# Order of the parts inside an attention step of a two-model transformer kernel

## The reference

```python
# first model: 8 heads of 64; with 256 tokens there is one block, so causal softmax
p = softmax(where(causal, (q*scale) @ k.T, -1e30)); out = p @ v
attn = head_rms_norm(out, g)

# second model, layer 0: 8 heads, two score maps of 64 each, values of 128
w = softmax(q1 @ k1.T) - lam * softmax(q2 @ k2.T); o = rmsnorm(w @ v) * (1 - lam_init)

# second model, layer 1: 8 query heads of 128 on 2 key/value heads, no mask
o = softmax(q @ k.T) @ v
```

## Time and profile before

| what | value |
|---|---|
| timed runs, median (lowest to highest) | 1385.19 us (1384.85 to 1385.59) |
| profiled execution | 1380.57 us |
| its span | 1378.8 us |
| TensorE busy | 1148.3 us, 83% |
| VectorE busy | 611.7 us, 44% |
| ScalarE busy | 540.8 us, 39% |
| chain that ended last | PE 58%, DMA 24%, DVE 9%, ACT 7%, issue 2% |
| first / second / third attention | about 164 to 206 / 755 to 842 / 1110 to 1146 us |
| experts | about 240 to 700 us |

### The profile page before, as it was taken

One profiled execution on the slowest core, in us unless ns is written; L12 is line 12 of the kernel. 1 busy time (PEld: TensorE's weight loads), 2 busy tenths in 40 slices (PEclk: granted clock), 3 DMA queues, 4 the chain that ended last, 5 costly groups with the idle time before them and its releaser, 6 DMA issues.

```text
span 1378.8 us, 22374 instructions
## 1 busy us (share of the span) xinstructions
PE 1148.3 (83%) x9627; PEld 916.8 (66%) x9627; DVE 611.7 (44%) x1363; ACT 540.8 (39%) x1203; POOL 0.2 (0%) x4
## 2 busy tenths in 40 slices
PE   6989998866656666555689989999999979999997
PEld 4867668543333444333357758899998758899997
DVE  4564664210100111110065756665555865655554
ACT  4554553211100110110154655555554754555553
POOL 0000000000000000000000000000000000000000
PEclk9999998998887898987899999999999999999999
DMA  9895846899999999999978646645545664655520
GB/s 392 340 357 222 350 190 244 332 427 428 428 424 428 424 427 427 427 426 427 428 311 323 217 182 224 247 182 184 184 145 210 235 236 183 245 184 184 184 92 31
DMA packets 29569, 397.53 MB, mean 288 GB/s; under 512 B 3480, under 2 KB 4888, under 8 KB 5400
## 3 DMA queue, kind: packets, MB, share of 16 engines
q1 hardware_dynamic: 29032, 395.72, 71.8%
q10 hardware_dynamic: 432, 0.30, 0.1%
HBM read 394.97 MB, written 1.05 MB: 287 GB/s over the span
## 4 chain that ended last, share of the span: by engine, by line
PE 58%; DMA 24%; DVE 9%; ACT 7%; issue 2%; ACTq 0%; DVEq 0%
PE ps L141 58%; DMA ring<-in_w 12%; DMA mem<-in_w 11%; DVE mem L141 4%; DVE memr L141 3%; ACT mem L141 3%; ACT memr L141 3%; DMA ring<-in_wpk 1%; DVE small L141 1%; DMA posi<-in_pos 1%; ACT L141 0%; ACT rowb L141 0%; DVE x L141 0%; DVE mcol L141 0%; ACTq L141 0%
## 5 line engine op out<-in xcount | busy, mean ns | idle before, releaser
L141 PE MATMUL ps<-memr 128*128 128x256 f32 (+1 forms) x4680 | 668.6, 302 | 17.9 <-DVE memr L141 17.9
L141 PEld LDWEIGHTS ps<-memr 128*128 128x128 f32 x4680 | 610.7, 192 | 62.4 <-DVE memr L141 27.7
L141 DVE TENSOR_TENSOR memr<-ring,memr 128x512 fp32r<-128x512 f32 x440 | 297.8, 691 | 245.3 <-ACT memr L141 242.0
L141 ACT ACTIVATE memr<-ring 128x512 fp32r<-128x512 f32 x440 | 268.3, 627 | 220.0 <-PE ps L141 212.3
L141 PE MATMUL ps<-mem 128*32 128x256 f32 (+4 forms) x2232 | 266.8, 407 | 59.9 <-DMA mem<-in_w 35.2
L141 ACT ACTIVATE mem<-ps 128x256 f32<-128x256 f32 (+5 forms) x307 | 121.3, 407 | 421.4 <-PE ps L141 419.4
L141 PEld LDWEIGHTS ps<-mem 128*32 128x32 f32 (+2 forms) x2232 | 172.8, 147 | 117.8 <-issue 59.5
L141 PE MATMUL ps<-ring,mem 128*32 128x256 f32 x1536 | 140.6, 432 | 75.6 <-DMA mem<-in_w 39.0
L141 PEld LDWEIGHTS ps<-ring,mem 128*32 128x32 f32 x1536 | 72.2, 124 | 122.4 <-issue 99.3
L141 DVE TENSOR_TENSOR mem<-mem,ps 128x256 f32<-128x256 f32 (+1 forms) x76 | 31.8, 418 | 270.7 <-ACT mem L141 270.6
L141 DVE COPY mem<-ps 32x256 f32<-32x256 f32 (+2 forms) x81 | 38.2, 471 | 114.9 <-PE ps L141 113.9
(11 more groups left out here) (91 smaller groups left out, 380.4 us busy)
## 6 DMA issues: line engine op xcount, KB each, us to landing
ring<-in_wpk SPq DMA_DIRECT2D x89, 2048.0 KB, 8.1
mem<-in_w SPq DMA_DIRECT2D x48, 2048.0 KB, 32.0
ring<-in_w SPq DMA_DIRECT2D x48, 2048.0 KB, 30.4
mem<-in_wpk SPq DMA_DIRECT2D x1, 2048.0 KB, 10.5
ring<-in_wpk SPq DMA_DIRECT2D x2, 1024.0 KB, 5.1
x<-in_x SPq DMA_DIRECT2D x2, 512.0 KB, 5.6
out_dram<-mem SPq DMA_DIRECT2D x4, 256.0 KB, 2.2
cst<-in_cst SPq DMA_DIRECT2D x1, 944.0 KB
```

The costliest lines, as they stand in the source:

```text
L141: ins = o[1](*o[2], **o[3])
```

## The change

In both generators the calls inside a step are put in another order. Before: scores, weigh, turn_e, values, finish. After, in the first attention: values, turn_e, finish, weigh, scores; in the second model's: values, turn_e, finish, weigh, scores as well. The conditions, the heads that each call works on, the parts themselves and the places of the steps between slabs stay.

```diff
@@ -1048,16 +1048,16 @@
                 uu_free[u] = c_r[ch]
 
             for s_ in range(12):
+                if 3 <= s_ < 11:
+                    values(s_ - 3)
+                if 2 <= s_ < 10:
+                    turn_e(s_ - 2)
+                if s_ >= 5 and s_ % 2:
+                    finish((s_ - 5) // 2)
+                if 1 <= s_ < 9:
+                    weigh(s_ - 1)
                 if s_ < 8:
                     scores(s_)
-                if 1 <= s_ < 9:
-                    weigh(s_ - 1)
-                if 2 <= s_ < 10:
-                    turn_e(s_ - 2)
-                if 3 <= s_ < 11:
-                    values(s_ - 3)
-                if s_ >= 5 and s_ % 2:
-                    finish((s_ - 5) // 2)
                 yield
 
 
@@ -1711,16 +1711,16 @@
             def attention():
 
                 for s_ in range(21):
+                    if s_ >= 4 and s_ % 2 == 0 and s_ < 20:
+                        values(s_ // 2 - 2)
+                    if 2 <= s_ < 18:
+                        turn_e(s_ - 2)
+                    if s_ >= 5 and s_ % 2:
+                        finish((s_ - 5) // 2)
+                    if 1 <= s_ < 17:
+                        weigh(s_ - 1)
                     if s_ < 16 and s_ % 2 == 0:
                         scores(s_ // 2)
-                    if 1 <= s_ < 17:
-                        weigh(s_ - 1)
-                    if 2 <= s_ < 18:
-                        turn_e(s_ - 2)
-                    if s_ >= 4 and s_ % 2 == 0 and s_ < 20:
-                        values(s_ // 2 - 2)
-                    if s_ >= 5 and s_ % 2:
-                        finish((s_ - 5) // 2)
                     yield
 
             at_ = attention()
```

## The result

The changed kernel takes 1396.52 us (median of 6 runs, 1394.26 to 1398.04), the old one beside it 1385.39 us. The ratio is 1.0077, 95% interval 1.0064 to 1.0089: 10.7 us slower (8.9 to 12.3); the two medians lie 11.1 apart. The profiled execution took 1396.07 us (span 1394.2).

What follows compares the result with a forecast made beforehand. Outside the transfer-paced expert part, time was taken to be lost where TensorE waits. Second attention +2.5, third +3.9, first +0.3 sum to +6.7 us on the 1385.19 median: 1391.9, range 1386.0 to 1397.0.

Steps and rivals of the forecast that it cites:

- rival A: More slow clock: one extra slow stretch each in the second and third attention, 1.4 us each, 1394.7 us; chance 0.18.
- Step 9 and 10 of the second attention: Scaling runs behind finish and ends at 806.95; step 10's transposes wait 2.4 us for it.
- The slab behind it: Second attention, step 10: transposes 0.2, scores 1.07, slab 1.65, ending at 809.95 instead of 808.4; 1.5 us lost.
- It is in the old time, and I leave one in the new: Second attention: one half-clock stretch behind steps 11 and 12, costing 1.4 us, stays in the new time.
- Step 12: Second attention: values at 812.1 after the turned copy, scaling behind finish at 815.25, scores end near 816.6; lag 1.0 us.
- The closed loop: Third attention: one head's chain from scores to transposes takes 4.6 us, against 2.45 between scores(4) and scores(5) before.
- Step 2's lag: First attention: scores now start behind the wait for scaling(0), before 1.09 us; loses 0.8 us.
- so the cadence stays: First attention: a pair of steps takes VectorE and ScalarE about as long in either order.
- the 1.40: First attention, step 9: the wait of 1.40 us shrinks, since 0.8 us of values go ahead of the transposes.
- Rivals B and C: B: faster, finish and values freed, 1380.8 us, chance 0.08. C: nothing to measure, gains and losses cancel, 1385.2, chance 0.12.
- The 0.71 us waits: Second attention: the finish product's 0.71 us waits for the square go, since the square no longer stands behind the exponentials.
- PSUM's banks: Banks taken in rotation change their order of use; taken as 0, bounds -0.5 and +1 us.

Runs made afterwards that it cites:

- e7: The whole change plus one to three idle-time products, results unread, ahead of TensorE's long waits in all three attentions; 9.0 us slower than the old kernel, ratio 1.0065.
- e8: The whole change, but step 12 of the second attention keeps the old order; 10.5 us slower than the old kernel, ratio 1.0076.
- e9: The old order plus one idle-time product ahead of step 11's transposes and one ahead of step 12's values, second attention; 2.8 us faster than the old kernel, ratio 0.9980.
- e1: The old kernel with only the first attention put in the changed order; 3.5 us slower, ratio 1.0025.
- e4b: All three attentions ordered values, turn, scaling, finish, scores: the change with scaling ahead of finish; 7.9 us slower than the old kernel, ratio 1.0057.
- e5: All three attentions ordered scores, values, turn, finish, scaling: scores first, the rest reversed; 3.5 us slower than the old kernel, ratio 1.0025.
- e2: The old kernel with only the second attention put in the changed order; 5.3 us slower, ratio 1.0038.
- e6: The old order with values ahead of scores in the first and second attention, except the second's step 12; 2.2 us slower than the old kernel, ratio 1.0016.
- e3: The old kernel with only the third attention put in the changed order; 3.9 us slower, ratio 1.0028.
- e10: As e9, plus values ahead of scores in the second attention except steps 11 and 12; 2.4 us faster than the old kernel, ratio 0.9983.

## Why the prediction was right, and where it was short

The side was right, and so was the place: slower, in the attentions. 1396.5 lies in the range, near its upper end, but above the forecast's own high end (near 1395): it is inside by the room left above rival A, not by the sum. The forecast of +6.7 us was 4 us short, and rival A (+9.5) came closest. By the timed runs of one attention each, +0.3 became +3.5, +2.5 became +5.3, and +3.9 was met.

- **Step 9 and 10 of the second attention.** Right, by 0.04 us for the end of the scaling and 2.01 us for a wait put at 2.4.
- **The slab behind it.** I put transposes, scores and slab of step 10 at 2.9 us. They took 811.37 + 2.78 - 809.51 = 4.6. The step that failed is "It is in the old time, and I leave one in the new": in the second attention there is a slow stretch behind each of the three waits of 2 us or more, not one in all. e7's trace puts the clock at 4.4 us of the second attention's 5.8 and 2.6 of the third's 6.1 (by e8's trace of the same code it would be 1.1); e9 shows such a price once, 1.7 us, and there the timed runs agree.
- **Step 12.** I let values wait for the turned copy only and missed that values(4) also wait for the copies of the value projection's second half, which ScalarE has behind the finish chain. So values came last and not the scaling: in the change the copies end at 817.74 and values start at 817.89. Transposes and scores queued behind them, and the units start 22.0 us behind step 8's start, forecast 816.6 - 797.83 = 18.8. In e7 it is 819.63 - 800.16 = 19.5, so 2.5 of the 3.2 us are clock. The other 0.7 is the late chain; e8, where values no longer stand in front, has 19.4, so their place costs little by itself.
- **Second attention in all.** +2.5 forecast, +5.8 measured, +1.4 with the idle products.
- **Third attention.** The closed loop was right, 4.6 us forecast and 4.80 measured (4.72 in e7); +3.9 forecast, +3.5 in e7's trace with the clock held at 1.00, +6.1 without. "The third attention has 1.00 throughout" was no promise for longer waits.
- **First attention.** Forecast +0.3 with bounds up to +1.5, measured +2.4 in the traces of three kernels (the change, e1, e8), and +2.2 with the idle products, so by e7's trace this is queue order and not clock. Step 2's lag was right (0.8; the wait grew from 1.09 to 1.93). The mis-sized term is "so the cadence stays": the lag of VectorE and ScalarE was not made good, steps 8 and 9 waited 1.60 and 1.30 us, and the 1.40 did not shrink by 0.8. e4b and e5 each win back 1.1 to 1.2 of it; how the rest splits is not settled.
- **Cause.** I gave finish the blame in the second attention. The experiments give the larger share to scores last: with scores first and finish still ahead of the scaling, the second attention lost 0.4 us of 5.8. Finish ahead of the scaling costs much only when the exponentials are late as well; with scores last it cost 3.1 us of the 5.8 in e4b's trace, clock included. So the part that I blamed is real, but it needs the other to bite.
- **Rivals B and C.** The 0.71 us waits did go, as B says, but each was worth less than the wait that followed. PSUM's banks I had at nothing; no run separates them.
- **Between the attentions.** I had these stages at nothing and called a change in them a sign of being wrong; they took +1.41 and +1.30 us. The second varies by as much without any relation to the order (267.6 to 270.6). The first doesn't: 551.2 in the change, e1 and e8 and 551.6 in e4b, which have scores last in the first attention, 549.7 to 550.0 in the seven kernels that have not, and 550.5 in e7, which has scores last but also the idle products. The 32 products ahead of the experts, behind the same wait of 1.98 us, take 7.05 us in the first three and 6.68 in e4b, in the other traces 4.85 to 5.81. So the first attention's order seems to reach past its end by way of the clock, in these single traces; how is open.

TensorE: Matmul & The Clock Gate, Part 1, of the Trainium skill says that idleness lowers the array's clock and steady work restores it. The traces agree: 0.50 at 818 us behind waits of 2.01 and 3.09 us, and 1.00 with the same waits filled. Which idleness is enough they don't settle, as e8's 2.57 us shows.

## What to carry to other kernels

In a software-pipelined step (each part works on what an earlier step left), queue first what starts the longest chain over the engines, here scores, maxima, exponentials: in this kernel the distance between producer and consumer in the queues is what hid the latency, and the first operation of a step should be one whose every record is old. Before a wait is taken as the cause, ask which wait comes next: with the scaling ahead of finish, 1.7 us of waiting vanished in step 10, and step 12's values, held by another record, still started 17.4 us behind step 8 instead of 17.6. A TensorE wait can cost twice, once by itself and once by the clock behind it, and its length alone didn't tell which waits did. In this kernel two products that nobody reads, put into such waits, made it faster, which no order of the parts that was tried alone did.

## What the runs showed of the hardware

- The length of a wait did not decide whether the clock fell behind it. Behind 1.93 us in the change's first attention a slab took 2.61 us instead of 1.7; behind 2.57 us in e8 and 2.03 us in e5's first attention everything ran at 1.00 (a slab in 1.68 us); behind 0.98 us in the third attention of e2 and e6 four products took 2.08 us, in the old kernel behind the same wait 1.13. Behind the same 1.58 us in the changed third attention they took 1.46 us in the change, 1.99 in e3, 1.10 in e8. What decides is open.
- The old code of the third attention was granted 1.00 in four traces, 0.96 in e2 and 0.92 in e6. The same instructions with the same waits took 41.80 to 44.39 us.
- The mean granted clock of a run goes with its time: of the 72 timed runs of the old kernel beside the experiments, the 14 with 0.938 or less took 1388.2 us on average, the 20 with 0.943 or more 1384.6.
- With one to three products of 128x512 in the waits the clock stayed at 1.00 in all three attentions of e7 and in the second of e9 and e10.
- The timed runs of one kernel scatter by up to 9 us (the old one 1380.5 to 1389.5 in one set of 23), while an attention's stage in two traces with the same code and the same granted clock agrees within 0.25 us. For changes of this size the stages told more than the medians, as long as the clock in them was read too.
